# A second prefetch place of 2 MB beside an eight-slot weight ring, both places used for two rounds

## The chip, the cores and the metric

One Trainium2 chip; the kernel runs on one of its cores. The metric is the device time of one execution, in microseconds. The kernel before takes 1180.39 us (median of three runs, 1180.38 to 1183.22).

## What is computed

A decoder layer on 256 tokens of width 1024, all in float32: RMSNorm, a combined input projection, an S5 state-space mixer and an RWKV-7 time mixer side by side, an output projection, then a mixture of 32 experts (the four best per token) with clamped SwiGLU, an input embedding p that is gated by the residual, and a last RMSNorm. The part around the change, cut to its core:

```
logits = h @ router_w + router_b
top_v, top_i = top_k(logits, 4);  gates = softmax(top_v)
for every expert e, for the tokens that chose it:
    gt  = min(x @ w_gate[e] + b_gate[e], 7)
    up  = clip(x @ w_up[e] + b_up[e], -7, 7)
    act = (up + 1) * gt * sigmoid(1.702 * gt)
    out[token] += (act @ w_down[e] + b_down[e]) * gate
x = x + out
x = x + (p @ ple_w_proj) * sigmoid(rms_norm(x) @ ple_w_gate)
result = rms_norm(x) * final_g
```

Every expert's three matrices (1024 x 1024 float32, 4 MB each, 402 MB in all) are read from HBM once.

## The kernel before

**Memory.** Nearly all on-chip memory is one tensor, arena, of 47 units; a unit is 128 partitions x 1024 float32 (512 KB). un(i, n) are n units from unit i. The mixers use the units for their own data first; the expert phase takes them over as they fall free. Small tensors beside it: rec, bb, cc, lora_hidden, s5p (20 x 16 columns), power (160) and coef (256), which hold the S5 mixer's tables and are dead when the experts begin.

**Chunks and the ring.** An expert's weights come as six chunks of 2 MB (four units): two of gate, two of up, two of down, chunk c of expert e in the order in which TensorE uses them. Chunk i below counts through all experts: 0 to 191. The ring has eight slots (NSLOT) at the units of RING. Beside it there is one special place, extra, made of units 24, 25, 26 and 29, which holds chunk 8 and is used once. So nine chunks are fetched before or as the first expert begins: chunks 0 to 7 into slots 0 to 7, and chunk 8.

**Who fetches.** All these transfers are issued by SyncE, in the order written in the block for sync and then in expert_sync; its queue is in order, and a wait holds everything behind it. Ahead of the experts it issues slots 0, 4, 5 (L335), the token rows and the p projection's weights, slot 1 (L348, when the RWKV chunks are done), slots 6 and 7 (L352, on mix_rw_ready), slots 2 and 3 (L355, when the output projection is done), and three of the four units of extra (L358, when the router's logits are done). The fourth unit, 29, holds the weights of the p projection until that is done; expert_sync issues it (L1490) after chunk 12, on ple_done 4. TensorE raises the semaphore chunks_used when it has used a chunk. In expert_sync chunk i waits for chunks_used i-8 up to chunk 16 and for i-7 from then on (L1487, then the loop at L1499, then L1502), and goes to slot (i-1) mod 8. Behind the last chunk, which is fetched in two halves, come the two chunks of ple_w_gate (L1510) and the final gain (L1512).

**TensorE per expert** (expert in expert_tensor). Gate: 16 matmuls of 64 rows x 512 columns for each of two chunks, then the bias; up the same; then scatter, which adds the output y of the expert before to the four banks of outputs (4 matmuls, with the gate weights gT turned for the scatter); two transposes of the gate table pg and four of the act; gather of the next expert's tokens (4 matmuls); the down matmuls of two chunks, with the turn of the gathered rows between them. VectorE does the clamps and the product (the act stage, L1562 to L1569), ScalarE the sigmoid and the copies. Every float32 matmul runs as two passes, and the trace counts passes. For expert 0 there is more: open_outputs does the second half of the p projection for bank 1 (ple_proj(1)), waits until ScalarE has copied it (L1343), and opens the four banks with the down biases; then scatter runs on y and gT, which VectorE cleared beforehand (L1388, L1389), so that it adds zeros.

## Time and profile before

| | |
|---|---|
| median of three runs | 1180.39 us |
| the profiled execution's own time | 1182.24 us |
| its span | 1180.4 us |
| TensorE matmul busy | 1104.3 us (94%) |
| VectorE, ScalarE busy | 359.5 us (30%), 198.6 us (17%) |
| bytes moved, mean rate | 430.58 MB, 365 GB/s |
| granted clock of TensorE | 0.998 |

The span runs from the first to the last recorded instruction; the own time is the device's time for the same execution. A busy share is a mean over stages with different limits, so what a change is worth has to be read in the stage that it touches. The granted clock 0.998 is that of the full level, 2.4 GHz.

### The profile page before, as it was taken

To read this page: it belongs to the slowest core of one execution; us is meant where nothing else is said; L and a number is where in the kernel's file an instruction comes from. 1 tells how busy PE (TensorE), PEld (TensorE's weight loads), DVE (VectorE), ACT (ScalarE), POOL (GpSimd) and SP (SyncE) were. 2 spreads that over 40 slices of the span, in tenths; PEclk is the share of its full clock that TensorE was granted. 3 is DMA by queue.
4 is the path that set the end of the run, shared out by engine and by line. 5 is a ranking of instruction groups with operands and counts; after the bars stand their busy time and mean duration, and the time that the engine had idled before them with its cause. 6 is when DMAs were issued, how large, how long until landed. Compare 5 with 4: busy or idle time off the path is not lost.

```text
span 1180.4 us, 16582 instructions
## 1 busy us (share of the span) xinstructions
PE 1104.3 (94%) x7042; PEld 480.1 (41%) x7042; DVE 359.5 (30%) x745; ACT 198.6 (17%) x318; POOL 5.8 (0%) x11
## 2 busy tenths in 40 slices
PE   9999999999999999999999999999999999999987
PEld 8788974433333333333333333333333333333334
DVE  7987745312222222212111222222111111111123
ACT  6761322310110000000000000000000000000022
POOL 0100000000000000000000000000000000000000
PEclk9999999999999999999999999999999999999999
DMA  9402284899999999999999999999999999999970
GB/s 325 134 2 78 88 328 154 362 393 401 428 428 428 428 427 429 429 428 428 429 429 429 428 428 429 429 428 428 429 429 428 428 428 431 428 426 428 428 300 36
DMA packets 44844, 430.58 MB, mean 365 GB/s; under 512 B 4992, under 2 KB 15616, under 8 KB 20096
## 3 DMA queue, kind: packets, MB, share of 16 engines
q1 hardware_dynamic: 44608, 429.40, 87.2%
q8 instruction: 36, 0.59, 0.2%
q0 software_dynamic: 192, 0.52, 0.1%
q14 instruction: 8, 0.07, 0.0%
HBM read 428.86 MB, written 1.05 MB: 364 GB/s over the span
## 4 chain that ended last, share of the span: by engine, by line
PE 50%; DMA 44%; DVE 4%; ACT 1%; issue 1%; SPq 0%; DVEq 0%; ACTq 0%
PE bank L1321 34%; DMA arena<-in_exp_w_up 24%; DMA arena<-in_exp_w_gate 19%; PE bank L249 13%; PE bank L1383 1%; DVE arena L638 1%; PE bank L1632 1%; PE bank L1628 1%; DMA arena<-in_xT 0%; ACT arena L475 0%; PE bank L984 0%; DVE arena L882 0%; DVE arena L629 0%; DVE arena L632 0%; PE bank L266 0%
## 5 line engine op out<-in xcount | busy, mean ns | idle before, releaser
L1321 PE MATMUL bank<-arena 128*64 128x512 f32 (+3 forms) x3808 | 849.7, 588 | 59.1 <-DMA arena<-in_exp_w_up 52.0
L1321 PEld LDWEIGHTS bank<-arena 128*64 128x64 f32 (+3 forms) x3808 | 272.4, 140 | 591.1 <-issue 471.6
L249 PE MATMUL bank<-arena 64*64 64x64 f32 (+8 forms) x2104 | 170.7, 265 | 7.1 <-issue 3.6
L249 PEld LDWEIGHTS bank<-arena 64*64 64x64 f32 (+3 forms) x2104 | 137.0, 146 | 35.9 <-issue 18.5
L1517 ACT ACTIVATE cc<-arena 128x512 f32<-128x512 f32 x32 | 20.2, 630 | 459.7 <-DVE arena L1562 459.7
L1567 DVE TENSOR_SCALAR arena<-bank 128x512 f32<-128x512 f32 x32 | 22.1, 692 | 219.9 <-PE bank L1321 219.9
L1364 DVE TENSOR_TENSOR arena<-bank,par 128x512 f32<-128x512 f32 x32 | 22.1, 692 | 216.7 <-PE bank L1383 216.7
L1562 DVE TENSOR_SCALAR arena<-bank 128x512 f32<-128x512 f32 x32 | 22.1, 692 | 163.4 <-PE bank L1321 163.4
L1522 ACT ACTIVATE arena<-bank 128x256 f32<-128x256 f32 x32 | 12.3, 383 | 313.9 <-PE bank L1628 313.9
L1577 DVE COPY arena<-bank 128x512 f32<-128x512 f32 x32 | 22.1, 692 | 98.7 <-PE bank L1321 98.7
L1377 ACT ACTIVATE rec<-bank 128x512 f32<-128x512 f32 x32 | 34.2, 1069 | 43.0 <-PE bank L1321 43.0
L1569 DVE SCALAR_TENSOR_TENSOR arena<-arena,cc 128x512 f32<-128x512 f32 x32 | 33.8, 1056 | 1.1
L1565 DVE TENSOR_TENSOR cc<-cc,arena 128x512 f32<-128x512 f32 x32 | 22.2, 692 | 24.5 <-ACT cc L1517 24.5
L1383 PEld LDWEIGHTS bank<-con,rec 128*128 128x128 f32 x128 | 13.4, 141 | 26.2 <-issue 25.1
L1383 PE MATMUL bank<-con,rec 128*128 128x128 f32 x128 | 21.0, 286 | 0.8 <-ACT rec L1377 0.8
L1524 ACT ACTIVATE arena<-bank 128x512 f32<-128x512 f32 x32 | 19.1, 597 | 1.7
L1549 DVE TENSOR_SCALAR arena<-con,arena 128x128 f32<-128x128 f32 x64 | 19.1, 341 | 0.9 <-issue 0.8
L1632 PE MATMUL bank<-con,arena 128*128 128x128 f32 x128 | 19.2, 273 | 0.0
L1360 DVE TENSOR_SCALAR arena<-con,arena,small 128x64 f32<-128x64 f32 x64 | 17.2, 311 | 6.7 <-DVE arena L1555 6.6
L1628 PEld LDWEIGHTS bank<-con,arena 128*128 128x128 f32 x64 | 6.4, 141 | 24.3 <-issue 24.3
L1632 PEld LDWEIGHTS bank<-con,arena 128*128 128x128 f32 x128 | 15.0, 140 | 0.0
L1628 PE MATMUL bank<-con,arena 128*128 128x128 f32 x64 | 14.0, 301 | 0.0
(278 smaller groups left out, 406.8 us busy)
## 6 DMA issues: line engine op xcount, KB each, us to landing
arena<-in_exp_w_gate SPq DMA_DIRECT2D x64, 2048.0 KB, 31.9
arena<-in_exp_w_down SPq DMA_DIRECT2D x63, 2048.0 KB, 35.4
arena<-in_exp_w_up SPq DMA_DIRECT2D x63, 2048.0 KB, 34.3
arena<-in_w_in SPq DMA_DIRECT2D x8, 1024.0 KB, 12.0
arena<-in_w_out SPq DMA_DIRECT2D x4, 1024.0 KB, 6.3
arena<-in_ple_w_gate SPq DMA_DIRECT2D x2, 2048.0 KB, 33.3
arena<-in_exp_w_down SPq DMA_DIRECT2D x2, 1024.0 KB, 34.5
arena<-in_exp_w_up SPq DMA_DIRECT2D x1, 1536.0 KB, 12.8
```

Of the source, the lines that this page charges most:

```text
L249: return nc.tensor.matmul(out, lhsT, rhs, start=start, stop=stop, skip_group_check=True)
L1321: return nc.tensor.matmul(out, lhsT, rhs, start=start, stop=stop, skip_group_check=True)
L1364: nc.vector.tensor_tensor(xg[:, :, :].rearrange("p (h k) s -> p k h s", h=2), GAT[:, :].rearrange("p (k h s) -> p k h s", h=2, k=4), prm(" ...
L1377: nc.scalar.activation(by_run(xc), plain(GAT[:, :]), ACT.Copy).then_inc(s["moved"], 1)
L1383: last = nc.tensor.transpose(GAT[:, k * P:(k + 1) * P], xc[:, k * P:(k + 1) * P], ident)
L1562: ts(gt, GATE[:, :], 7.0, None, ALU.min).then_inc(s["gt_ready"], 1)
L1565: tt(sg, sg, gt, ALU.mult).then_inc(s["swish_ready"], 1)
L1567: ts(up, UP[:, :], 7.0, -7.0, ALU.min, ALU.max).then_inc(s["swish_ready"], 1)
L1569: stt(by_run(gt), plain(up), 1.0, plain(sg), ALU.add, ALU.mult).then_inc(s["act_ready"], 1)
L1577: V.tensor_copy(y, YB[:, :]).then_inc(s["y_ready"], 1)
L1628: ins = nc.tensor.transpose(YB[:, t * P:(t + 1) * P], pg[:, t, :], ident)
L1632: ins = nc.tensor.transpose(GATE[:, k * P:(k + 1) * P], gt[:, k * P:(k + 1) * P], ident)
```

## The change

- There are two special places instead of one. Place a is units 24 to 27, place b units 37, 38, 28, 29. In the first round they hold chunks 8 and 9, in the second 18 and 19. FIRST is 10, the number of places.
- Chunks 0 to 9 fill the ten places, 10 to 19 fill them again, and chunks 20 to 27 go to the eight slots. Up to chunk 27 chunk i waits for chunks_used i-9; from chunk 28 on the ring alone is used and chunk i waits for i-7, in slot (i-20) mod 8, which is (i-4) mod 8. Chunk 28 thus waits for three uses more than chunk 27.
- Units 37 and 28 of place b are fetched right behind slot 1, unit 38 behind slots 2 and 3, the whole of place a where three units of extra went, and unit 29 behind chunk 11, still on ple_done 4. Chunk 19 is fetched in two pieces of 1 MB.
- To free the units, the routing state moves: gates, ranks and counts to power, one-hot, pick and turned gates to s5p, gT to coef, pg, up and the gathered rows xc to rec, the four p projections to bb, lora_hidden and unit 40, xg and the routing scratch to unit 41, y to the place of the down bias, half of the turned rows x2T to unit 24.
- Expert 0's scatter of zeros is left out, with the clearing of gT and y; the second part of the p projection moves from open_outputs to just behind the gate bias of expert 0.
- The final gain goes to unit 43 and is fetched one use later.

The diff, cut where it only passes names on or gives tiles other columns:

```diff
-        x2T = [feat(25 + 3 * (k // 4))[:, k % 4, :] for k in range(KD)]
+        x2T = [feat(25 - k // 4)[:, k % 4, :] for k in range(KD)]
-        extra = [un(a) for a in (24, 25, 26, 29)]
+        extra = [[un(a) for a in places] for places in ((24, 25, 26, 27), (37, 38, 28, 29))]
...
-        ahead = chunk_src(NSLOT % NC, 1)
+        ple = [bb.rearrange("p m n -> p (m n)"), lora_hidden[:, :], un(40)[:, 0:512], un(40)[:, 512:1024]]
+        ahead = [chunk_src((NSLOT + i) % NC, 1) for i in range(2)]
...
                 sp.dma_start(slot(1), chunk_src(1, 0)).then_inc(chunk_in[1], 16)
+                for k, place in ((0, 37), (2, 28)):
+                    sp.dma_start(un(place), ahead[1][:, k * D:(k + 1) * D]).then_inc(extra_in[1], 16)
...
                 for c in (2, 3):
                     sp.dma_start(slot(c), chunk_src(c, 0)).then_inc(chunk_in[c], 16)
+                sp.dma_start(un(38), ahead[1][:, D:2 * D]).then_inc(extra_in[1], 16)
                 sp.wait_ge(s["logits_done"], 1)
                 sp.wait_ge(s["x2_root"], 2)
-                sp.dma_start(un(24, 3), ahead[:, 0:3 * D]).then_inc(extra_in, 16)
+                sp.dma_start(un(24, 4), ahead[0]).then_inc(extra_in[0], 16)
...
-        V.memset(gT[:, :, :], 0.0).then_inc(s["gT_ready"], 1)
-        V.memset(y, 0.0).then_inc(s["y_ready"], 1)
-        for i, name in enumerate(("actT_ready", "gT_done")):
+        for i, name in enumerate(("gT_ready", "y_ready", "actT_ready", "gT_done")):
             V.memset(st[:, 8 + i:9 + i], 0.0).then_inc(s[name], 1)
...
     def open_outputs(pe):
 
-        ple_proj(1, banks[1]).then_inc(mixer["ple_done"], 1)
         pe.wait_ge(s["ple_copied"], 4)
         for n in range(4):
-            mm(banks[n][:, :], gatesT[rows[n], :], bias_down[rows[n], :], True, False)
+            last = mm(banks[n][:, :], gatesT[rows[n], :], bias_down[rows[n], :], True, False)
+        return last
...
+    FIRST = NSLOT + len(extra)
+    def ring_slot(i):
+        return (i - 2 * FIRST) % NSLOT
...
     def expert_sync(sp):
-        for i in range(NSLOT + 1, QUAD * NC):
-            sp.wait_ge(s["chunks_used"], i - NSLOT if i <= 2 * NSLOT else i - NSLOT + 1)
-            sp.dma_start(slot((i - 1) % NSLOT), chunk_src(i % NC, i // NC)).then_inc(chunk_in[(i - 1) % NSLOT], 16)
-            if i == NSLOT + 4:
+        for i in range(FIRST, 2 * FIRST + NSLOT):
+            sp.wait_ge(s["chunks_used"], i - FIRST + 1)
+            src = chunk_src(i % NC, i // NC)
+            if i == 2 * FIRST - 1:
+                sp.dma_start(un(37, 2), src[:, 0:2 * D]).then_inc(extra_in[1], 16)
+                sp.dma_start(un(28, 2), src[:, 2 * D:4 * D]).then_inc(extra_in[1], 16)
+            elif i == 2 * FIRST - 2:
+                sp.dma_start(un(24, 4), src).then_inc(extra_in[0], 16)
+            else:
+                c = i % FIRST if i < 2 * FIRST else ring_slot(i)
+                sp.dma_start(slot(c), src).then_inc(chunk_in[c], 16)
+            if i == FIRST + 1:
                 sp.wait_ge(mixer["ple_done"], 4)
-                sp.dma_start(extra[3], ahead[:, 3 * D:4 * D]).then_inc(extra_in, 16)
+                sp.dma_start(un(29), ahead[1][:, 3 * D:4 * D]).then_inc(extra_in[1], 16)
...
+        begun = 2 * FIRST + NSLOT - QUAD * NC
         with sp.Fori(1, n_last) as q:
-            for i in range(QUAD * NC):
-                if i % NC == 0:
+            for i in range(begun, begun + QUAD * NC):
+                if i % NC == 0 or i == begun:
                     e = sp.snap((QUAD * q + i // NC) % E)
                 sp.wait_ge(s["chunks_used"], QUAD * NC * q + (i - NSLOT + 1))
-                sp.dma_start(slot((i - 1) % NSLOT), chunk_src(i % NC, e)).then_inc(chunk_in[(i - 1) % NSLOT], 16)
+                sp.dma_start(slot(ring_slot(i)), chunk_src(i % NC, e)).then_inc(chunk_in[ring_slot(i)], 16)
...
-        sp.wait_ge(s["chunks_used"], base + (2 * QUAD * NC - 5))
+        sp.wait_ge(s["chunks_used"], base + (2 * QUAD * NC - 4))
         sp.dma_start(fg[:, :], io["final_g"].to_broadcast([P, D])).then_inc(t2["fg_in"], 16)
...
                 ins.then_inc(s[done], 1)
+                if q is None and place == 0 and m == 0:
+                    ple_proj(1, banks[1]).then_inc(mixer["ple_done"], 1)
             if q is None and place == 0:
-                open_outputs(pe)
-            pe.wait_ge(s["gT_ready"], n + 1)
-            pe.wait_ge(s["y_ready"], n + 1)
-            scatter().then_inc(s["scattered"], 1)
+                open_outputs(pe).then_inc(s["scattered"], 1)
+            else:
+                pe.wait_ge(s["gT_ready"], n + 1)
+                pe.wait_ge(s["y_ready"], n + 1)
+                scatter().then_inc(s["scattered"], 1)
```

The order on SyncE from slot 1 to chunk 15, with the semaphores waited for. 128x4096 is a chunk, 128x1024 a unit. Before:

```order
L348 DMA arena<-in_exp_w_gate 128x4096 [waits state_done,y_done,u0_done]
L352 DMA arena<-in_exp_w_gate 128x4096 [waits mix_rw_ready]
L352 DMA arena<-in_exp_w_gate 128x4096
L355 DMA arena<-in_exp_w_up 128x4096 [waits out_done]
L355 DMA arena<-in_exp_w_up 128x4096
L358 DMA arena<-in_exp_w_up 128x3072 [waits x2_root,logits_done]
L1487 DMA arena<-in_exp_w_up 128x4096 [waits m_chunks_used]
L1487 DMA arena<-in_exp_w_down 128x4096 [waits m_chunks_used] x2
L1487 DMA arena<-in_exp_w_gate 128x4096 [waits m_chunks_used]
L1490 DMA arena<-in_exp_w_up 128x1024 [waits ple_done]
L1487 DMA arena<-in_exp_w_gate 128x4096 [waits m_chunks_used]
L1487 DMA arena<-in_exp_w_up 128x4096 [waits m_chunks_used] x2
```

Now:

```order
L350 DMA arena<-in_exp_w_gate 128x4096 [waits state_done,y_done,u0_done]
L352 DMA arena<-in_exp_w_up 128x1024 x2
L356 DMA arena<-in_exp_w_gate 128x4096 [waits mix_rw_ready]
L356 DMA arena<-in_exp_w_gate 128x4096
L359 DMA arena<-in_exp_w_up 128x4096 [waits out_done]
L359 DMA arena<-in_exp_w_up 128x4096
L360 DMA arena<-in_exp_w_up 128x1024
L363 DMA arena<-in_exp_w_up 128x4096 [waits x2_root,logits_done]
L1508 DMA arena<-in_exp_w_down 128x4096 [waits m_chunks_used] x2
L1511 DMA arena<-in_exp_w_up 128x1024 [waits ple_done]
L1508 DMA arena<-in_exp_w_gate 128x4096 [waits m_chunks_used] x2
L1508 DMA arena<-in_exp_w_up 128x4096 [waits m_chunks_used] x2
```

Two units move up to a place without a wait of their own, one unit to a place behind slot 3, and chunk 9 no longer waits for a use.

The order on TensorE in expert 0, from the up matmuls' first chunk (chunk_in2) to the transposes of the act. Before:

```order
L1321 MATMUL bank<-arena 64x512 [waits chunk_in2]
L1321 MATMUL bank<-arena 64x512 x7
L1321 MATMUL bank<-arena 64x512 [waits chunk_in3]
L1321 MATMUL bank<-arena 64x512 x7
L1321 MATMUL bank<-arena 64x512 [waits m_gatesT_ready,bias_split,m_picked]
L1321 MATMUL bank<-arena 64x512
L249 MATMUL bank<-arena,lora_hidden 128x512 x2
L1321 MATMUL bank<-arena 128x512 [waits m_ple_copied]
L1321 MATMUL bank<-arena 128x512 x3
L1321 MATMUL bank<-arena 128x512 [waits m_y_ready,m_gT_ready]
L1321 MATMUL bank<-arena 128x512 x3
L1628 MATMUL bank<-con,arena 128x128 [waits m_pg_ready]
```

Now:

```order
L249 MATMUL bank<-arena,lora_hidden 128x512 x2
L1327 MATMUL bank<-arena 64x512 [waits chunk_in2]
L1327 MATMUL bank<-arena 64x512 x7
L1327 MATMUL bank<-arena 64x512 [waits chunk_in3]
L1327 MATMUL bank<-arena 64x512 x7
L1327 MATMUL bank<-arena,s5p 64x512 [waits m_gatesT_ready,bias_split,m_picked]
L1327 MATMUL bank<-arena,s5p 64x512
L1327 MATMUL bank<-arena,s5p 128x512 [waits m_ple_copied]
L1327 MATMUL bank<-arena,s5p 128x512 x3
L1658 MATMUL bank<-con,rec 128x128 [waits m_pg_ready]
```

The p projection stands ahead of the up matmuls, and the four matmuls that waited for y and gT are gone.

## Rows read from the trace of the kernel before

**Rows 1.** The page, part 2: GB/s moved, in 40 equal slices of the span.
```profile
GB/s 325 134 2 78 88 328 154 362 393 401 428 428 428 428 427 429 429 428 428 429 429 429 428 428 429 429 428 428 429 429 428 428 428 431 428 426 428 428 300 36
```

**Rows 2.** The chain that ended last, in order of time: start, us, what.
```profile
471.56 35.25 DMA arena<-in_exp_w_up
...
1088.18 35.88 DMA arena<-in_exp_w_up
1124.10 5.79 PE bank L1321 x26
...
1148.73 22.36 PE bank L1321 x64
```

**Rows 3.** Windows: busy us of each engine (x count), granted clock, DMA share, GB/s.
```profile
184.00:190.00 6.00, 6.00 (x15) 2.66 (x14) 4.15 (x3) 2.94 (x4) 0.00 (x0) 1.00 0.95 344
190.00:200.00 10.00, 8.72 (x21) 3.60 (x20) 9.73 (x19) 0.00 (x0) 0.00 (x0) 1.00 0.01 3
200.00:204.00 4.00, 4.00 (x17) 2.27 (x16) 1.77 (x3) 1.88 (x5) 0.00 (x0) 1.00 1.03 336
204.00:224.00 20.00, 17.48 (x94) 10.37 (x94) 7.20 (x31) 11.40 (x29) 0.00 (x0) 1.00 1.00 427
224.00:228.00 4.00, 4.00 (x22) 1.36 (x20) 1.39 (x7) 0.00 (x0) 0.00 (x0) 1.00 0.07 28
228.00:248.00 20.00, 19.31 (x92) 6.75 (x90) 3.14 (x4) 3.27 (x5) 0.00 (x0) 1.00 1.00 410
248.00:252.00 4.00, 4.00 (x22) 1.45 (x20) 0.69 (x1) 0.00 (x0) 0.00 (x0) 1.00 0.84 258
252.00:276.00 24.00, 24.00 (x117) 8.21 (x114) 5.12 (x12) 2.68 (x4) 0.00 (x0) 1.00 0.99 414
276.00:288.00 12.00, 12.00 (x60) 4.31 (x62) 3.37 (x10) 0.02 (x1) 0.00 (x0) 1.00 0.93 356
288.00:460.00 172.00, 172.00 (x826) 60.43 (x822) 37.49 (x81) 18.73 (x28) 0.00 (x0) 1.00 1.01 428
460.00:1100.00 640.00, 588.58 (x2747) 195.68 (x2743) 128.20 (x286) 56.90 (x85) 0.00 (x0) 1.00 1.01 428
```

**Rows 4.** The timeline of SyncE's issues: start, us, engine, line, out<-in.
```profile
183.40 0.34 SPq L348 DMA_DIRECT2D arena<-in_exp_w_gate  x1
199.08 0.81 SPq L352 DMA_DIRECT2D arena<-in_exp_w_gate  x2
213.46 0.33 SPq L358 DMA_DIRECT2D arena<-in_exp_w_up  x1
227.15 0.33 SPq L1487 DMA_DIRECT2D arena<-in_exp_w_up  x1
249.64 0.33 SPq L1487 DMA_DIRECT2D arena<-in_exp_w_gate  x1
267.76 0.33 SPq L1487 DMA_DIRECT2D arena<-in_exp_w_down  x1
276.00 0.33 SPq L1487 DMA_DIRECT2D arena<-in_exp_w_gate  x1
1114.97 0.43 SPq L1512 DMA_DIRECT2D arena<-in_final_g  x1
```

**Rows 5.** The timeline of TensorE over experts 0 and 1; x counts passes.
```profile
223.45 14.39 PE L1321 MATMUL bank<-arena 128*64 128x512 f32 x68 [0.78 <-DVE arena L1364]
237.77 1.98 PE L249 MATMUL bank<-arena,lora_hidden 128*128 128x512 f32 x4
240.44 3.06 PE L1321 MATMUL bank<-arena 32*128 32x512 f32 x16 [0.69 <-ACT arena L1343]
250.12 19.74 PE L1321 MATMUL bank<-arena 128*64 128x512 f32 x92
...
276.48 19.74 PE L1321 MATMUL bank<-arena 128*64 128x512 f32 x92
```

**Rows 6.** DMA issues of the page: KB each, us to landing.
```profile
arena<-in_exp_w_up SPq DMA_DIRECT2D x63, 2048.0 KB, 34.3
```

More of the change, by code:

```diff
@@ L291, in slot @@
             return un(RING[c], RUN)
-        ahead = chunk_src(NSLOT % NC, 1)
-        clear_expert_state, rest_sync, rest_scalar, rest_vector, rest_tensor = experts(nc, io, ctx, arena, con, par, banks, ring, slot, ahead, extra, sg, xc, chunk_in, extra_in, chunk_src, p_in, ple_proj, s, logits, inv, by_run, plain, x2, bias_parts, bias_down, rbias)
+        ple = [bb.rearrange("p m n -> p (m n)"), lora_hidden[:, :], un(40)[:, 0:512], un(40)[:, 512:1024]]
+        state_tables = [a.rearrange("p m n -> p (m n)") for a in (s5p,)] + [a.rearrange("p a b n -> p (a b n)") for a in (power, coef)]
+        ahead = [chunk_src((NSLOT + i) % NC, 1) for i in range(2)]
+        clear_expert_state, rest_sync, rest_scalar, rest_vector, rest_tensor = experts(nc, io, ctx, arena, con, par, banks, ring, slot, ahead, extra, sg, rec, ple, state_tables, chunk_in, extra_in, chunk_src, p_in, ple_proj, s, logits, inv, by_run, plain, x2, bias_parts, bias_down, rbias)
         with nc.Block() as block:
@@ L1263, in _, with experts @@
                 rest_tensor(pe)
-def experts(nc, io, ctx, arena, con, par, banks, ring, slot, ahead, extra, sg, xc, chunk_in, extra_in, chunk_src, p_in, ple_proj, mixer, logits, inv, by_run, plain, x2, bias_parts, bias_down, rbias):
+def experts(nc, io, ctx, arena, con, par, banks, ring, slot, ahead, extra, sg, rec, ple, state_tables, chunk_in, extra_in, chunk_src, p_in, ple_proj, mixer, logits, inv, by_run, plain, x2, bias_parts, bias_down, rbias):
     def sb(name, shape, dt=F32):
@@ L1281, in experts @@
     HF = D // 2
-    y = un(40)[:, 0:HF]
-    xg = un(40)[:, HF:2 * HF].rearrange("p (k s) -> p k s", k=KD)
+    tables, counts, turned_gates = state_tables
+    xc, up = rec[:, 0:HF], rec[:, 0:HF]
+    pg = rec[:, HF:HF + TT * P].rearrange("p (t m) -> p t m", t=TT)
+    y = bias_down
     gt = un(41)[:, 0:HF]
-    up = un(41)[:, HF:2 * HF]
+    xg = un(41)[:, HF:2 * HF].rearrange("p (k s) -> p k s", k=KD)
     actT = un(42)[:, HF:2 * HF].rearrange("p (h k s) -> p k h s", h=2, k=4)
-    gT = un(37)[:, 0:TT * P].rearrange("p (t m) -> p t m", t=TT)
@@ L1307, in experts @@
-    nbase = un(38)[:, 425:426].bitcast(I32)
-    nlast = un(38)[:, 426:427].bitcast(I32)
+    gT = turned_gates.rearrange("p (t m) -> p t m", t=TT)
+    onehot = tables[:, 0:128].rearrange("p (t m) -> p t m", t=TT)
+    pick = tables[:, 128:160].bitcast(BF16)
+    gatesT = tables[:, 160:288]
+    st = tables[:, 288:320]
+    gates = counts[:, 0:64].rearrange("p (t e) -> p t e", t=TT)
+    rank = counts[:, 64:128].rearrange("p (t e) -> p t e", t=TT)
+    cnt, cflag = counts[:, 128:136], counts[:, 136:144]
@@ new lines, in experts @@
+    nbase = counts[:, 145:146].bitcast(I32)
+    nlast = counts[:, 146:147].bitcast(I32)
+    route = un(41)[:, 256:1024]
+    lg = route[:, 0:64].rearrange("p (t e) -> p t e", t=TT)
+    mask = route[:, 64:128].rearrange("p (t e) -> p t e", t=TT)
+    top = route[:, 128:144].rearrange("p (t e) -> p t e", t=TT)
+    topi = route[:, 144:160].bitcast(U32).rearrange("p (t e) -> p t e", t=TT)
+    topf = route[:, 160:176].rearrange("p (t e) -> p t e", t=TT)
+    ex = route[:, 176:192].rearrange("p (t e) -> p t e", t=TT)
@@ L1332, in chain @@
         return link
-    ple = [un(28 - n // 2)[:, (n % 2) * HF:(n % 2 + 1) * HF] for n in range(4)]
     PLE_ORDER = (2, 3, 0, 1)
```

65 lines of the change are left out of this document (29 added, 36 removed).

## The prediction

> **What bounds the kernel now.** I read the throughput of the transfers slice by slice first. From the eleventh slice (295 us) to the end of the expert phase every slice shows 426 to 431 GB/s [rows 1]: the transfer engines never rest, and nothing in TensorE's work changes that rate. Next the chain that ended last, in order of time: until 471 us it runs through TensorE alone, from there through transfers of expert weights with TensorE between them, as in the first piece shown and the last one, which hands over at 1124.10 us; behind it stands the tail, whose gate matmuls take 22.36 us [rows 2]. So the end is set by when the chunk that lands at 1124 lands. It is the 190th of 192 (chunk 189, the second half of the last expert's up matrix). All bytes ahead of it pass through one queue in order, so its time is the moment the stream starts, plus bytes over rate, plus every microsecond in which the stream stood still for want of a free place. The windows show where it stood still: almost nothing moves in 190 to 200, 28 GB/s in 224 to 228, 258 in 248 to 252, 414 in 252 to 276, 356 in 276 to 288, then 428 throughout [rows 3]. TensorE is busy for 172.00 us of the 172 from 288 to 460, and 588.58 of the 640 after that [rows 3]: it first lives on the buffered lead and then waits for data. One chunk of 2048 KB [rows 6] at 428.4 GB/s (between the 428 and 429 of [rows 1]) takes 4.90 us, an expert's six 29.4 us; TensorE needs 26.36 (250.12 to 276.48, [rows 5]).
>
> So one question prices this change: how much of the stream's idle time before 288 us does it fill, and does it open new idle time later. A microsecond saved on TensorE is worth something only if it releases a place that the stream waits for.
>
> **What the stream loses now.** Against 428.4 GB/s: 204 to 224: 0.07 us; 224 to 228: 3.74; 228 to 248: 0.86; 248 to 252: 1.59; 252 to 276: 0.81; 276 to 288: 2.03 [rows 3]. Together 9.1 us. The causes are in SyncE's issues [rows 4]. The special place's 1.5 MB went out at 213.46; the next chunk can only go when chunk 0 is used, at 227.15. Chunk 13 waited for the fifth use, at 249.64. Chunk 18 waited for use 11, at 276.00, a whole act stage behind use 10 at 267.76, and since chunk 17 is where the distance had fallen from nine places to eight, nothing was queued. A model with one queue, a start 1.7 us behind the issue (issue at 199.08; the 336 GB/s of 200 to 204 are 3.14 us at full rate, so data starts at 200.86, [rows 3, 4]) and 4.90 us a chunk gives a gap at each of these three places: 4.8, 1.6 and 2.0 us, 8.4 in all. The 0.8 us of 252 to 276 it doesn't explain.
>
> **The change, part by part.**
>
> 1. *Two units (1 MB) of the second special place go out right behind chunk 1, at 183.8 us.* No wait stands between (the order of SyncE). Chunk 1's data ends at 190 (344 GB/s over 184 to 190 are its 2.1 MB), and the stream then rests until 200.86 [rows 3]. 1 MB is half a chunk, 2.45 us: it fits into that rest. **Gain 2.45 us.** Nobody reads those units before the expert phase, and slots 6 and 7 still go out at 199.08.
>
> 2. *Unit 38 goes out behind slots 2 and 3, and the first special place takes 2 MB at 213.46 instead of 1.5.* The stream from 200.86 carries 6, 7, 2, 3, a quarter chunk, and a whole one: 5.25 chunks or 25.7 us, to 226.6, where before it ended at 224.1. The next data starts at 228.8 (use at 227.15 and 1.7). The gap is 2.3 us where the model had 4.8: **2.5 us saved**. The bytes are no extra ones; they come out of the work behind.
>
> 3. *Ten places until chunk 27.* Chunk i now waits for use i-9 where it waited for i-8 (from 17 on i-7). Stream from 228.8: chunks 10 to 13 and the quarter chunk of unit 29 end at 249.6. Chunk 14 now needs the fifth use, which was at 249.64 and comes at 247.5 (point 4); with 1.7 us that is 249.2, so **the 1.6 us gap is gone**, with 0.4 us to spare. Chunk 20 (use 11, at 273.9) meets a stream busy until 283.9: **the 2.0 us gap is gone**. Without point 4 the first of these would keep about 1.7 us.
>
> 4. *The first expert on TensorE.* Left out: the scatter of zeros, 8 passes of 0.214 us (92 passes in 19.74 us, [rows 5]), 1.7 us. The p projection (1.98 us) moves ahead of the up matmuls, so the 0.69 us wait for ScalarE's copy of it [rows 5] is gone too: ScalarE copies it behind the sigmoid, during the up matmuls. Uses 3 and 4 come 1.95 us later, which costs the stream nothing, as chunk 11 is queued ahead until 238.6. Uses 5 and later come 2.4 us earlier, less some 0.3, my estimate for what now shows of VectorE's act: the scatter was covering it, and the opening matmuls (3.06 less 1.7 us) and two transposes alone are short of it. I take 2.1. TensorE's own saving is worth nothing at the end, since transfers set it; it counts only through point 3.
>
> 5. *The ring falls from ten to eight at chunk 28.* This is the new wait: chunk 27 goes at use 18, chunk 28 only at use 21. Use 11 was at 276.00; use 23 is two periods of 26.36 later, 328.7; use 21 is the act stage (276.00 less 267.76, 8.24 us) and one chunk (16 passes, 3.4) before that, 317.1, and 315.0 with point 4. Chunk 27 ends at 228.8 + 18.25 x 4.90 = 318.2. Data for 28 can flow from 316.7, so it is in time by 1.5 us. Chunk 30 waits for use 23, 326.6 + 1.7 = 328.3, and 29 ends at 328.0: a gap of **0.3 us lost**. Behind it the lead of TensorE shrinks by 3 us an expert, uses come ahead of the stream's need, and no gap follows. Bounds for this step: nothing, and 2.0 us (what the same fall from nine to eight costs now).
>
> 6. *At nothing.* State in other tables: the same instructions on VectorE and ScalarE, with two memsets fewer, at about 199 us, where TensorE has its own work (8.72 us of the ten from 190, 4.00 of the four from 200, [rows 3]). up and the gathered rows share rec: the one is written after the other has been turned, as TensorE's order has it anyway. Final gain one use later (now issued at 1114.97, [rows 4]): it stands in the queue behind the last weights, of which 4.25 chunks follow the one that lands at 1124.10, so it comes by about 1145, and the tail needs it behind its gate matmuls, at 1171 [rows 2]. One more loop step on SyncE: transfers there are issued some seven chunks ahead of landing (34.3 us, [rows 6]).
>
> Row and rule differ on the small pieces. In 204 to 224 the stream crosses from one transfer to the next four times and moves 427 GB/s [rows 3], so a border costs under 0.1 us when the next one is queued. The Trainium skill (SBUF — State Buffer, The DMA setup-cost knee) says that every transfer pays a fixed 2 us or so, and to coalesce into the largest; there are three transfers more than before (eight for chunks 8, 9, 18 and 19 instead of five), which by that figure would be an estimate of 6 us of the gain. The page itself puts most of it down to completion, which a queued successor covers; the trace agrees.
>
> **The sum.** Early megabyte 2.45, first gap 2.5, second 1.6, third 2.0, less 0.3: 8.2 us; I take 8.1, since chunk 14 comes so close. The unexplained 0.8 stays. Bounds: 2.45 + 2.5 = 4.9 if the later dips stay, and 2.45 + 9.1 - 2.3 = 9.2 if all but the first gap's rest goes. The profiled execution took 1182.24 us, so the sum is 1174.1 against it; it lay 1.85 above the median of the three runs, 1180.39, and against that the forecast is **1172.3 us**, 0.7% faster. About 0.3%, 3.5 us, is what a measurement of this kernel can tell from no change.
>
> **Rivals.**
> - *The dips stay* (20%). The losses at 248 to 288 come from a queue one or two deep at each issue, not from missing places, or the fall at chunk 28 costs its 2.0 us. For it: 0.8 us that my model can't place, and margins of 0.4 and 1.5 us at chunks 14 and 28. Against: three gaps fit the issues to 0.1 us. Gain 4.9: 1175.5.
> - *The early megabyte isn't early* (3%): the change doesn't do what it says, because something holds SyncE there or the transfers run beside slots 6 and 7. Gain 8.1 - 2.45: 1174.7. Against: SyncE has nothing to wait for there.
> - *Each piece pays* (8%). Three more transfers take 2 us of the stream each. A start of 1.7 us behind an issue is in the rows, but only when the stream was empty. Gain 8.1 - 6: 1178.3, no change. This is the knee of the Trainium skill's page named above, taken literally.
> - *More* (5%): all of the dips go; 9.2 gained: 1171.2.
> - *The stream slows* (4%), the case on the other side. Chunk i now goes to slot (i-4) mod 8 instead of (i-1) mod 8, for all of the long stretch. The 186 chunks from 200.86 to the last that counts take 911 us; a rate 0.9% lower eats the 8.1 us, and from there on the kernel is slower: at 420 GB/s it loses 18 us, 1190. Against: 426 to 431 in every slice, whatever the phase between matrix and slot [rows 1].
>
> **Chances.** Forecast, a gain of 7 to 9: 60%. Faster by over 0.3% takes the forecast, the dips, the late megabyte and the larger gain: 88%; within 0.3%: 8%; slower: 4%. The range reaches from 1170.0 (the larger gain and a microsecond of scatter) to 1176.8 (the dips stay, and a microsecond), which leaves out the last two cases, 12%, and the edges.
>
> **What would show it.** In the changed profile: transfers busy at 190 to 193; 336 GB/s or so still in 200 to 204; the low window of 224 to 228 about half as deep; full rate through 248 to 288; at most a small dip at 328; chunk 14 issued at about 247.5; TensorE's first wait for weights later than 471, and the last weight transfer of the chain handing over at 1116 instead of 1124.10, with the tail behind it unchanged. Wrong would be: a dip of over 1 us at 315 to 330 (point 5), one at 247 to 252 (point 4), or a rate under 428 behind 330 us (the last rival).

## The result, and the profile after

| | before | changed |
|---|---|---|
| median of five runs each | 1183.22 us (1180.38 to 1183.46) | 1174.35 us (1172.43 to 1175.17) |
| profiled execution, own time | 1182.24 us | 1174.35 us |
| its span | 1180.4 us | 1172.6 us |

The ratio is 0.9931, with a 95% interval of 0.9917 to 0.9945: 8.1 us of the before's 1180 or so (6.5 to 9.8 by the interval), and 7.9 between the two profiled executions. The forecast was a gain of 8.1 us and a time of 1172.3. The median of before rose from 1180.39 with two more runs, both near 1183.4; its five values lie near 1180.4 and near 1183.3. The last section shows how far such differences can be followed.

The page's GB/s in 40 slices, for the changed kernel, answers to [rows 1]:

```profile
GB/s 323 138 2 43 84 369 173 395 414 428 428 425 428 426 428 427 429 429 429 428 429 429 427 428 429 429 429 429 428 429 428 428 429 429 427 427 428 428 296 36
```

The full rate begins a slice earlier; the plateau behind it is where it was, with one slice of 425. The windows answer to [rows 3] (busy us of PE, PEld, DVE, ACT, POOL, then granted clock, DMA share, GB/s):

```profile
190.00:200.00 10.00, 8.72 (x21) 3.67 (x20) 9.79 (x20) 0.00 (x0) 0.00 (x0) 1.00 0.28 111
200.00:204.00 4.00, 4.00 (x17) 2.20 (x16) 1.00 (x2) 1.95 (x5) 0.00 (x0) 1.00 0.97 340
204.00:224.00 20.00, 17.48 (x94) 10.43 (x94) 7.20 (x31) 11.36 (x29) 0.00 (x0) 1.00 1.01 426
224.00:228.00 4.00, 4.00 (x22) 1.30 (x20) 1.39 (x7) 0.00 (x0) 0.00 (x0) 1.00 0.66 283
228.00:248.00 20.00, 19.56 (x94) 6.65 (x90) 3.13 (x4) 3.28 (x5) 0.00 (x0) 1.00 1.00 410
248.00:252.00 4.00, 4.00 (x21) 1.37 (x21) 0.80 (x2) 0.00 (x0) 0.00 (x0) 1.00 0.97 369
252.00:276.00 24.00, 24.00 (x118) 8.52 (x116) 5.71 (x13) 2.69 (x4) 0.00 (x0) 1.00 1.00 422
276.00:288.00 12.00, 12.00 (x60) 4.03 (x58) 3.37 (x10) 0.63 (x1) 0.00 (x0) 1.00 1.02 431
320.00:332.00 12.00, 12.00 (x60) 4.33 (x58) 2.26 (x5) 2.06 (x3) 0.00 (x0) 1.00 1.00 422
460.00:1100.00 640.00, 592.68 (x2774) 198.51 (x2772) 127.78 (x286) 59.08 (x88) 0.00 (x0) 1.00 1.01 428
```

Read each against 428.4 GB/s, as the prediction did. 190 to 200 now moves 1.1 MB where nothing moved. 224 to 228 loses 1.36 us instead of 3.74, 228 to 248 0.86 as before, 248 to 252 0.55 instead of 1.59, 252 to 276 0.36 instead of 0.81, 276 to 288 nothing instead of 2.03, and there is a new 0.18 in 320 to 332. With 0.11 in 204 to 224 that is 3.4 us where 9.1 were lost; with the megabyte in the earlier rest (2.45) the stream stands 8.1 us ahead.

SyncE's issues answer to [rows 4]:

```profile
183.72 0.91 SPq L352 DMA_DIRECT2D arena<-in_exp_w_up  x2
199.02 0.80 SPq L356 DMA_DIRECT2D arena<-in_exp_w_gate  x2
213.40 0.33 SPq L363 DMA_DIRECT2D arena<-in_exp_w_up  x1
227.09 0.33 SPq L1508 DMA_DIRECT2D arena<-in_exp_w_down  x1
247.71 0.33 SPq L1508 DMA_DIRECT2D arena<-in_exp_w_up  x1
274.07 0.33 SPq L1508 DMA_DIRECT2D arena<-in_exp_w_up  x1
315.34 0.36 SPq L1521 DMA_DIRECT2D arena<-in_exp_w_down  x1
326.98 0.33 SPq L1521 DMA_DIRECT2D arena<-in_exp_w_gate  x1
```

These are the two early units, slots 6 and 7, place a, and chunks 10, 14, 20, 28 and 30. TensorE's timeline in expert 0 answers to [rows 5]:

```profile
230.62 1.98 PE L249 MATMUL bank<-arena,lora_hidden 128*128 128x512 f32 x4
232.54 7.09 PE L1327 MATMUL bank<-arena 128*64 128x512 f32 x32
239.46 1.46 PE L1327 MATMUL bank<-arena,s5p 128*64 128x512 bf16 x10
240.84 0.44 PE L1658 MATMUL bank<-con,rec 128*128 128x128 f32 x2
241.72 0.66 PE L1662 MATMUL bank<-con,arena 128*128 128x128 f32 x4 [0.44 <-DVE arena L1592]
```

The scatter is gone, and 0.44 us of VectorE's act shows in its place. The chain that ended last, in order of time, answers to [rows 2]:

```profile
515.62 31.33 DMA arena<-in_exp_w_gate
...
1080.79 35.40 DMA arena<-in_exp_w_up
1116.20 0.04 issue
1116.24 5.79 PE bank L1327 x26
...
1140.87 22.36 PE bank L1327 x64
```

TensorE lives on its lead 44 us longer, and the last weight transfer hands over 7.86 us earlier (1124.10 to 1116.24). Everything behind it takes what it took: 22.36 us of gate matmuls, and 24.63 us from the handover to their start, before and after.

### The profile page after: what moved, and what is told of

Read it like the earlier page. It is cut to its first block, busy times and chain, and to the rows that moved or that the text cites. A ratio compares the mean times of both kernels' runs of the same rounds, so it can differ in the third digit from the quotient of the medians.

```text
span 1172.6 us, 16567 instructions
## 1 busy us (share of the span) xinstructions
PE 1102.4 (94%) x7034; PEld 481.8 (41%) x7034; DVE 358.3 (31%) x745; ACT 199.2 (17%) x318; POOL 5.4 (0%) x11
## 4 chain that ended last, share of the span: by engine, by line
PE 52%; DMA 41%; DVE 4%; ACT 1%; issue 1%; SPq 0%; DVEq 0%; ACTq 0%
PE bank L1327 37%; DMA arena<-in_exp_w_up 21%; DMA arena<-in_exp_w_gate 20%; PE bank L249 12%; PE bank L1388 1%; DVE arena L643 1%; PE bank L1662 1%; PE bank L1658 1%; DMA arena<-in_xT 0%; PE bank L989 0%; ACT arena L480 0%; DVE arena L887 0%; DVE arena L634 0%; DVE arena L637 0%; PE bank L266 0%
## 5 line engine op out<-in xcount | busy, mean ns | idle before, releaser
L1327 PE MATMUL bank<-arena 128*64 128x512 f32 (+1 forms) x3152 | 715.2, 593 | 52.1 <-DMA arena<-in_exp_w_up 46.6
L1327 PEld LDWEIGHTS bank<-arena 128*64 128x64 f32 (+1 forms) x3152 | 227.0, 138 | 503.2 <-issue 397.9
L1327 PE MATMUL bank<-arena,s5p 128*64 128x512 f32 (+2 forms) x392 | 87.7, 532 | 1.0 <-DVE s5p L1365 1.0
L1590 DVE TENSOR_SCALAR rec<-bank 128x512 f32<-128x512 f32 x32 | 22.1, 692 | 215.6 <-PE bank L1327 215.6
L1585 DVE TENSOR_SCALAR arena<-bank 128x512 f32<-128x512 f32 x32 | 22.1, 692 | 164.3 <-PE bank L1327 164.3
L1327 PE MATMUL bank<-arena,coef 64*128 64x512 f32 x256 | 63.6, 615 | 0.8 <-DVE arena L1600 0.8
L1327 PEld LDWEIGHTS bank<-arena,s5p 128*64 128x64 f32 (+2 forms) x392 | 23.3, 128 | 43.5 <-issue 42.4
L1327 PEld LDWEIGHTS bank<-arena,coef 64*128 64x128 f32 x256 | 22.0, 186 | 36.1 <-issue 34.5
L1592 DVE SCALAR_TENSOR_TENSOR arena<-rec,cc 128x512 f32<-128x512 f32 x32 | 33.7, 1052 | 1.1
L1572 DVE TENSOR_SCALAR rec<-con,power 128x128 f32<-128x128 f32 x64 | 19.1, 342 | 0.7 <-issue 0.7
```

Source lines behind the costliest of these rows:

```text
L1327: return nc.tensor.matmul(out, lhsT, rhs, start=start, stop=stop, skip_group_check=True)
L1585: ts(gt, GATE[:, :], 7.0, None, ALU.min).then_inc(s["gt_ready"], 1)
L1590: ts(up, UP[:, :], 7.0, -7.0, ALU.min, ALU.max).then_inc(s["swish_ready"], 1)
L1592: stt(by_run(gt), plain(up), 1.0, plain(sg), ALU.add, ALU.mult).then_inc(s["act_ready"], 1)
```

## The experiments

Twelve runs follow, and their expectations speak of three theories. **Theory 1**: the time is set by the *last* moment at which the stream of weight transfers stands still, since all that comes behind flows at one rate. **Theory 2**: each rest is priced by itself, and a microsecond of a filled one counts in full, as my prediction had it. **Theory 3**: TensorE's saved work is the gain.

One measure serves for all. Executions differ by some us in when the experts begin (last section), so I take from each profile the time from the issue of slots 6 and 7 to the handover of the last weight transfer of the chain. The changed kernel has 917.22 us (199.02 to 1116.24), the kernel before 925.02 (199.08 to 1124.10). Ratios are of the runs' times to those of the kernel before, with the 95% interval.

| run | issue | handover | us between | against the changed kernel | ratio |
|---|---|---|---|---|---|
| before | 199.08 | 1124.10 | 925.02 | +7.8 | 1 |
| changed | 199.02 | 1116.24 | 917.22 | 0 | 0.9931 |
| changed, again | 197.58 | 1114.65 | 917.07 | -0.2 | 0.9935 [0.9922, 0.9948] |
| early megabyte late | 198.75 | 1116.11 | 917.36 | +0.1 | 0.9934 [0.9920, 0.9948] |
| part 4 undone | 197.66 | 1116.52 | 918.86 | +1.6 | 0.9957 [0.9943, 0.9971] |
| before with part 4 | 197.22 | 1119.70 | 922.48 | +5.3 | 0.9983 [0.9973, 0.9993] |
| fall at chunk 18 | 197.72 | 1120.62 | 922.90 | +5.7 | 0.9997 [0.9979, 1.0016] |
| nine places | 198.59 | 1120.42 | 921.83 | +4.6 | 0.9972 [0.9956, 0.9987] |
| gather twice, expert 0 | 200.76 | 1119.08 | 918.32 | +1.1 | 0.9941 [0.9917, 0.9966] |
| gather twice, experts 4 to 30 | 199.21 | 1115.85 | 916.64 | -0.6 | 0.9938 [0.9916, 0.9960] |
| three rounds | 200.40 | 1118.53 | 918.13 | +0.9 | 0.9939 [0.9926, 0.9952] |
| three rounds, halves | 206.75 | 1124.05 | 917.30 | +0.1 | 0.9936 [0.9920, 0.9952] |
| two rounds, halves | 198.57 | 1115.62 | 917.05 | -0.2 | 0.9916 [0.9892, 0.9939] |
| unintended repeat | 197.30 | 1114.29 | 916.99 | -0.2 | 0.9930 [0.9908, 0.9952] |

Three profiles of the same changed kernel lie within 0.23 us in this measure. Every other kernel has one profile, and between kernels the measure can be off by more. The handover comes when chunk 189 has landed, and how much of what is queued behind it has been moved by then differs. Windows of 45 us from the handover on, in which the queue runs empty, for the changed kernel, the gather twice in experts 4 to 30, and three rounds:

```profile
1116.24:1161.24 45.00, 42.58 (x160) 20.28 (x161) 11.34 (x18) 8.86 (x15) 0.00 (x0) 1.00 0.42 171
1115.85:1160.85 45.00, 42.58 (x160) 20.31 (x161) 11.33 (x18) 8.85 (x15) 0.00 (x0) 1.00 0.44 178
1118.53:1163.53 45.00, 42.50 (x160) 20.35 (x161) 11.27 (x18) 8.85 (x15) 0.00 (x0) 1.00 0.41 166
```

171 GB/s over 45 us are 7.7 MB still to come; 7 GB/s more are 0.3 MB, so that handover comes 0.7 us early against the stream, and the last one, with 5 less, 0.5 us late. The kernel before and the other runs have 169 to 173, except the gather twice in expert 0 (176), before with part 4 (178) and three rounds with halves (165). Why the handover shifts stays open. So for small differences I also read how far the stream itself got: its rate over the 120 us that begin 25 us behind the issue of slots 6 and 7. It is 416, 416 and 417 GB/s in the three profiles of the changed kernel; 1 GB/s there is 0.28 us. The changed kernel, the gather twice in expert 0, and in experts 4 to 30:

```profile
224.02:344.02 120.00, 119.56 (x572) 41.56 (x568) 26.06 (x61) 11.98 (x18) 0.00 (x0) 1.00 0.99 416
225.76:345.76 120.00, 119.56 (x572) 41.45 (x568) 26.07 (x61) 11.95 (x18) 0.00 (x0) 1.00 0.99 409
224.21:344.21 120.00, 119.57 (x572) 41.42 (x569) 26.07 (x61) 11.96 (x18) 0.00 (x0) 1.00 0.99 415
```

**The changed kernel again.** The first is the yardstick.

> The changed kernel again, as the measure for the other runs of this call: 1172.4 to 1175.2 us, 8 us under the kernel before; the transfers rest in 226.6 to 228.8 and for 0.3 to 0.5 us at 328, and the last weight transfer of the chain hands over at 1116.2.

917.07 us against 917.22; as expected.

**The early megabyte, late.** The two unit loads move, still ahead of the first use:

```diff
                 sp.dma_start(slot(1), chunk_src(1, 0)).then_inc(chunk_in[1], 16)
-                for k, place in ((0, 37), (2, 28)):
-                    sp.dma_start(un(place), ahead[1][:, k * D:(k + 1) * D]).then_inc(extra_in[1], 16)
...
                 sp.dma_start(un(38), ahead[1][:, D:2 * D]).then_inc(extra_in[1], 16)
+                for k, place in ((0, 37), (2, 28)):
+                    sp.dma_start(un(place), ahead[1][:, k * D:(k + 1) * D]).then_inc(extra_in[1], 16)
```

> The early megabyte (units 37 and 28) moved behind slots 2 and 3, still ahead of the first use. Theory 1 (the last gap of the stream decides, here chunk 30, which waits for use 23): the megabyte fills the rest at 226.6 to 228.8 instead of the one at 190, the gap at 328 stays, handover at 1116.2, no change against the changed kernel. Theory 2 (the sum of my prediction: the early megabyte is worth 2.45 us by itself): 2.45 us slower, handover at 1118.7. Theory 3 (TensorE's saved work is the gain): no change either.

Measured: 917.36, and a ratio of 0.9934 beside the 0.9935 of the changed kernel. Its windows show why, against those of the changed kernel above:

```profile
190.00:200.00 10.00, 8.72 (x21) 3.60 (x20) 9.79 (x19) 0.00 (x0) 0.00 (x0) 1.00 0.09 16
...
224.00:228.00 4.00, 4.00 (x22) 1.39 (x20) 1.16 (x7) 0.00 (x0) 0.00 (x0) 1.00 1.03 438
228.00:248.00 20.00, 19.57 (x96) 6.66 (x94) 3.12 (x4) 3.28 (x5) 0.00 (x0) 1.00 1.01 429
```

The megabyte that is missing at 190 fills the rest at 224 to 228. Both rests lie ahead of the first use, and all ten places are full by then either way. Theory 2 falls: the early issue by itself is worth nothing that can be seen. What falls is the price put on one rest before the run. The rests of a finished profile may well be added up, as in the section above, since the stream's end is its bytes and its rests; but filling one rest can open or fill another.

**Part 4 undone.**

```diff
     def open_outputs(pe):
+        ple_proj(1, banks[1]).then_inc(mixer["ple_done"], 1)
         pe.wait_ge(s["ple_copied"], 4)
...
-                if q is None and place == 0 and m == 0:
-                    ple_proj(1, banks[1]).then_inc(mixer["ple_done"], 1)
             if q is None and place == 0:
-                open_outputs(pe).then_inc(s["scattered"], 1)
-            else:
-                pe.wait_ge(s["gT_ready"], n + 1)
-                pe.wait_ge(s["y_ready"], n + 1)
-                scatter().then_inc(s["scattered"], 1)
+                open_outputs(pe)
+            pe.wait_ge(s["gT_ready"], n + 1)
+            pe.wait_ge(s["y_ready"], n + 1)
+            scatter().then_inc(s["scattered"], 1)
```

gT is cleared again, and unit 29 goes behind chunk 12, so that SyncE doesn't stand in front of it.

> Part 4 of the change undone alone: the scatter of zeros is back in expert 0 and the p projection stands behind the up matmuls again. Theory 1: use 5 and all later ones come 2.1 us later, so chunk 30 starts at 330.4 instead of 328.3: 2.0 us slower than the changed kernel, handover at 1118.2, and rests of 1.7 us at 250 and 0.7 us at 330. Theory 2 says the same size, by the second gap (1.6) and more of the last. Theory 3: also about 2 us slower. If only the places mattered: no change.

1.6 us slower than the changed kernel, a fifth under the expected 2.0, with the rest at 250 back (343 GB/s in 244 to 252). Over its 120 us the stream moves 409 GB/s instead of 416, which is 2.0 us. So a saving of TensorE time in expert 0 is worth nearly its full size. The times alone can't tell the two kernels apart: their intervals overlap.

**The kernel before with part 4 alone.** The same edit the other way round, on the kernel before.

> The kernel before with part 4 alone (scatter of zeros left out, p projection ahead of the up matmuls). Theory 1: chunk 18 waits for use 11, which comes 2.1 us earlier: handover at 1122.1 instead of 1124.1, 2.0 us faster than before; the gap at 249 goes and the one at 276 stays as long. Theory 2 (gaps are added up): 1.6 us. If only the places mattered: no change.

2.5 us faster than before (925.02 to 922.48; ratio 0.9983, interval 0.9973 to 0.9993). Theory 1 said 2.0, theory 2 1.6, which is too close to choose between them. 0.7 of the 2.5 are the early handover (178 against the 171 of the kernel before); over the 120 us the stream moves 404 GB/s where it moved 397, which is 2.0 us. Part 4 is thus worth about 2 us on either kernel; the places are worth the other 5 to 6.

**The fall at chunk 18.** Everything as in the changed kernel, but both places count for one round only:

```diff
-            sp.wait_ge(s["chunks_used"], i - FIRST + 1)
+            sp.wait_ge(s["chunks_used"], i - FIRST + 1 if i < FIRST + NSLOT else i - NSLOT + 1)
```

> The changed kernel, but the distance falls from ten to eight at chunk 18 instead of 28 (chunks 18 to 27 wait two uses longer), as if both places were used for one round. Theory 1: chunk 18 waits for use 11 as in the kernel before, so all of the first round's lead is lost and only part 4 is left: 6 us slower than the changed kernel (2 us faster than before), handover at 1122.2, with one rest of 6.5 us at 269 to 276. Theory 2: the first gap and the megabyte (4.9 us) and the second (1.6) are kept, the third (2.0) comes back: 2 us slower than the changed kernel. Theory 3: no change.

This is where the theories lay furthest apart: theory 1 expected +6, theory 2 +2, theory 3 nothing. Measured +5.7. Windows and issues of this run:

```profile
248.00:268.00 20.00, 20.00 (x98) 7.05 (x96) 5.12 (x12) 1.55 (x3) 0.00 (x0) 1.00 1.00 414
268.00:276.00 8.00, 8.00 (x42) 2.75 (x38) 0.69 (x1) 1.14 (x2) 0.00 (x0) 1.00 0.39 124
276.00:288.00 12.00, 12.00 (x60) 3.99 (x58) 3.37 (x10) 0.63 (x1) 0.00 (x0) 1.00 0.98 401
```

```profile
257.45 0.33 SPq L1508 DMA_DIRECT2D arena<-in_exp_w_down  x1
272.77 0.33 SPq L1505 DMA_DIRECT2D arena<-in_exp_w_gate  x1
```

Chunk 17 goes at 257.45, chunk 18 only at 272.77, on use 11, and the stream, which was ahead, rests: 268 to 276 loses 5.7 us (8 x (1 - 124/428.4)). From there on it is where the kernel before would be with part 4: 922.90 and 922.48. All that the second place had won by 227 is given back at the next fall. **Without the second round the second place is worth nothing**, and this is the plainest finding of the study.

**Nine places.** Place b's first three units are fetched only on use 1, and chunk i waits for i-8 until 25 (their three loads ahead of the experts are taken out, which is not shown):

```diff
...
+        sp.wait_ge(s["chunks_used"], 1)
+        for k, place in ((0, 37), (1, 38), (2, 28)):
+            sp.dma_start(un(place), ahead[1][:, k * D:(k + 1) * D]).then_inc(extra_in[1], 16)
         for i in range(FIRST, 2 * FIRST + NSLOT):
-            sp.wait_ge(s["chunks_used"], i - FIRST + 1)
+            sp.wait_ge(s["chunks_used"], i - FIRST + 2 if i < 2 * FIRST + NSLOT - 2 else i - NSLOT + 1)
```

> One special place instead of two in effect: place b's first three units are fetched only after use 1, chunk i waits for i-8 until chunk 25 and for i-7 from 26 on. Nine places for two rounds. Theory 1: no rest at 249 worth naming (0 to 0.9 us), none at 276, the first rest is 3.5 us: 4.1 us slower than the changed kernel, handover at 1120.3. Theory 3: no change.

4.6 us slower than the changed kernel, half a microsecond over theory 1's 4.1. A place held for two rounds is worth about what it holds when the first use comes: one chunk, which takes 4.90 us.

**The gather twice in expert 0, and in experts 4 to 30.** The same added work (8 passes, same result) at two places of the program:

```diff
-                gather()
+                gather(2 if q is None and place == 0 else 1)
```

```diff
-                gather()
+                gather(1 if q is None else 2)
```

> The changed kernel with the gather of the next expert's tokens done twice in expert 0 (same result, 8 passes more, 1.7 us of TensorE). Theory 1: all uses from the fifth on 1.7 us later, chunk 30 starts 1.7 us later: 1.7 us slower, handover at 1117.9. Theory 3 (TensorE's work counts as work): 1.7 us too; it is told apart by the next run.

> The gather done twice in experts 4 to 30 instead (27 x 1.7 = 46 us of TensorE's work added), none in the first four. Theory 1: chunk 30 waits for a use of expert 3, everything later has slack: no change, handover at 1116.2, TensorE's waits for data shorter by 46 us. Theory 3: 46 us slower, or at least the part that fell into TensorE's own stretch until 515 us, some 15 us.

In expert 0 it costs 1.1 us by the handover (expected 1.7). Chunk 30 goes 1.72 us later after slots 6 and 7 (330.44 - 200.76 against 326.98 - 199.02), and the stream is behind by 7 GB/s over its 120 us, or 2.0 us; the handover then comes 0.5 us early against the stream (176 against 171). So the stream did move as theory 1 said, and a little over half a microsecond is lost in the measure. In 27 later experts, 46 us of added work in all, it costs nothing: 916.64, 0.6 less, which is the 0.7 of its early handover. Two more windows of that run:

```profile
288.00:460.00 172.00, 172.00 (x825) 60.37 (x822) 36.69 (x80) 16.20 (x25) 0.00 (x0) 1.00 1.01 426
460.00:1100.00 640.00, 627.52 (x2983) 217.55 (x2981) 127.92 (x286) 60.97 (x91) 0.00 (x0) 1.00 1.01 428
```

TensorE is busy 627.52 us of 640 where it was 592.68, and the stream moves its 428 GB/s as before. Theory 3 falls. Work on TensorE counts in expert 0, ahead of the use that the last held-up chunk waits for, and not at all in experts 4 to 30, behind it. It is free there because TensorE stays the faster side: its 26.36 us an expert with 1.7 more are still under the stream's 29.4. Where between expert 0 and expert 4 the border lies isn't shown; the run meant for it (the last one) didn't do what it should.

**Three rounds.**

```diff
     def ring_slot(i):
-        return (i - 2 * FIRST) % NSLOT
+        return (i - ROUNDS * FIRST) % NSLOT
...
-        for i in range(FIRST, 2 * FIRST + NSLOT):
+        for i in range(FIRST, ROUNDS * FIRST + NSLOT):
...
-        for place in range(QUAD):
+        for place in range(PEELED * QUAD):
             expert(None, place, NC * place)
```

with ROUNDS 3, PEELED 2, TensorE's loop from 2, and the final gain in unit 20.

> Both places used for three rounds; the distance falls at chunk 38; eight experts instead of four are written out ahead of TensorE's loop. Theory 1: the gap of 0.3 to 0.5 us at 328 goes and none comes at 365: handover at 1115.8, 0.4 us faster than the changed kernel, hardly to be told from it by the times.

A miss: 0.9 us slower than the changed kernel in the profile, where 0.4 less was expected; the times (0.9939) can't tell. 0.5 of it is the late handover (166 against 171). The page counts 0.66 MB of instructions fetched instead of 0.59, which at the stream's rate would be 0.2 us. The stream itself is where it was, 416 GB/s over its 120 us, so neither a loss nor the expected 0.4 shows in it.

**Halves.** Chunks 10 and 14 are fetched in two pieces, the first as soon as half of chunk 0 or of chunk 4 has been used:

```diff
         for i in range(FIRST, ROUNDS * FIRST + NSLOT):
+            if i in HALVED:
+                sp.wait_ge(half_used, 2 + HALVED.index(i) + 1)
+                sp.dma_start(slot(i % FIRST)[:, 0:2 * D], chunk_src(i % NC, i // NC)[:, 0:2 * D]).then_inc(half_in, 16)
...
+                    if q is None and place == 0 and m == 0 and k == RUN // 2 - 1:
+                        ins.then_inc(half_used, 1)
```

> As the one before, and chunks 10 and 14 are fetched in halves, the first as soon as TensorE has used half of chunk 0 and of chunk 4, so that the stream restarts 1.7 us earlier after the first fill. Theory 1: the rest at 226.6 shrinks from 2.3 to 0.6 us, small ones of 0.2 to 0.5 us at 232 and 253: handover at 1114.7, 1.5 us faster than the changed kernel (about 9.5 us under the kernel before). If pieces of 1 MB cost the stream something of their own: no gain.

> The changed kernel (two rounds) with chunks 10 and 14 in halves. From the issue of slots 6 and 7 to the handover of the last weight transfer the changed kernel takes 917.2 us. Theory 1 (the last rest of the stream decides; it is chunk 30's, bound to use 23): the rest at 227 shrinks by 1.7 us and the one at 328 grows by as much: 917.2, no change. Theory 2 (rests are added up): 915.5.

With three rounds it was to be 1.5 us faster than the changed kernel, and by the handover it is level with it: a miss. It is 0.8 us faster than three rounds without halves, where 1.1 was expected, and its stream moves 420 GB/s over the 120 us instead of 416, so it is 1.1 us ahead; the handover doesn't show that, coming late against the stream (165 against 171).

With two rounds: 917.05, no change. Windows of this run first, then those of the changed kernel; 223.57 and 224.02 are both 25 us behind the issue of slots 6 and 7:

```profile
223.57:231.57 8.00, 8.00 (x37) 2.66 (x32) 2.08 (x8) 0.56 (x1) 0.00 (x0) 1.00 0.91 311
248.00:252.00 4.00, 4.00 (x20) 1.29 (x18) 1.10 (x2) 0.00 (x0) 0.00 (x0) 1.00 0.95 403
320.00:340.00 20.00, 20.00 (x100) 7.18 (x100) 4.21 (x12) 2.68 (x4) 0.00 (x0) 1.00 1.00 413
```

```profile
224.02:232.02 8.00, 8.00 (x38) 2.65 (x32) 2.09 (x8) 0.56 (x1) 0.00 (x0) 1.00 0.82 311
320.00:340.00 20.00, 20.00 (x100) 7.05 (x98) 4.45 (x12) 2.69 (x4) 0.00 (x0) 1.00 1.00 420
```

The first rest did not shrink: 311 GB/s over these 8 us in either kernel, where 1.7 us less of rest was expected. The first half goes out 1.72 us before the second, but while the two halves pass, the stream is below its rate (295 GB/s in 228 to 232, against 336 in the changed kernel). What did change is small: 248 to 252 loses 0.24 us instead of 0.55, and 320 to 340 loses 0.72 instead of 0.39, so what is won ahead of chunk 30 is waited away at it. That agrees with theory 1, but since the first rest stayed as long, the run is no test of theory 2's 915.5. In the run with three rounds the same 8 us move 355 GB/s against 315 without halves, 0.7 us won of the expected 1.7. Why the halves run slowly there stays open.

No kernel of the study is clear of the changed one. The ratio 0.9916 of the run with two rounds is the lowest, but its interval holds the changed kernel's, and the measure within the profile is level.

**An edit that did nothing.** The last run was to add the same gather in expert 3:

```diff
-                gather()
+                gather(2 if q is None and place == QUAD - 1 else 1)
```

> The changed kernel with the gather done twice in expert 3, ahead of its down matmuls and so ahead of use 23. Theory 1: chunk 30 goes out 1.7 us later: 918.6 to 918.9 from the issue of slots 6 and 7 to the handover, against 917.2, though the same work in the 27 experts behind cost nothing. If the first gap alone decided: 917.2.

In expert, place counts chunks (0, 6, 12, 18), not experts, so the condition is never true and the kernel is the changed one. Chunk 30 goes out 127.96 us after slots 6 and 7 in both. The expectation is unanswered; the run counts as a third profile of the changed kernel, 916.99.

## Why the prediction was right, point by point

- **Total.** Forecast 8.1 us; 7.9 between the profiled executions, 8.1 by the ratio. The time itself came out at 1174.35 where 1172.3 was forecast: the gain was taken off 1180.39, a median of three runs, and five runs have theirs at 1183.22. Taken off the profiled execution it would have been 1174.1.
- **What bounds the kernel.** Right: no experiment moved the time clear of its scatter except by moving the stream, and 46 us of TensorE work were free.
- **Points 1 and 2, the early megabyte (2.45) and the first gap (2.5).** Their sum, one chunk, is right; taken apart they are wrong. Late, the megabyte fills the first gap instead, and nothing is lost. So the rival "the early megabyte isn't early" was mispriced: it would have given the same time as the forecast, not 1174.7. The step that failed is the one that priced a rest by itself.
- **The lower bound, too.** "The dips stay" was given a gain of 4.9 us, as if what is won at the first rest could be kept while a later one stays. With the fall at chunk 18, where the rest at 276 stays in just that way, the gain is 2.1 us (925.02 to 922.90), nearly all of it part 4's. The sum came out right because hardly any rest is left behind those that were filled, and point 5 had worked that out, with its gap of 0.3 and its margin of 1.5 us.
- **Point 3, ten places until chunk 27.** Use 5 was expected at 247.5 and chunk 14 went at 247.71; chunk 20 was expected at 273.9 and went at 274.07. 0.55 us remained at 248 to 252, where 0.4 to spare were forecast. It cost nothing in the end, because a later rest took its place.
- **Point 4, expert 0.** I took 2.1 us for use 5; it came 1.9 earlier (249.64 to 247.71), with 0.44 us of VectorE's act showing where I had 0.3. Its worth by experiment is 1.6 to 2.5 us by the handover, and 2.0 by the stream on either kernel: about a quarter of the whole gain, though I wrote only that the second gap "would keep about 1.7".
- **Point 5, the fall from ten to eight.** Chunk 28 was expected at 315.0 and went at 315.34, chunk 30 at 326.6 and 326.98; 0.18 us are lost in 320 to 332 and 0.39 in 320 to 340, where 0.3 was forecast. What I did not see is its rank. This is the rest that everything ahead is measured against: the gain is the distance by which the last rest moved. Chunk 18's data began at 277.7 in the kernel before, and twelve chunks later, at 336.5, would have been chunk 30's turn; it now begins at about 328.7 (326.98 and the same 1.7). The difference is 7.8 us, without any sum over gaps.
- **The 0.8 us that I couldn't place** in 252 to 276 halved to 0.36 by itself. Its cause stays open.
- **The start of 1.7 us.** It is a sum, not a pause: the rows of the kernel before, where chunk 9 is issued at 227.15, show no bytes until 228.00 and the first right after it, and then a rate that climbs; together that counts as 1.7 us. "Data starts at 200.86" is to be read in the same way.

```profile
227.50:228.00 0.50, 0.50 (x6) 0.15 (x4) 0.00 (x0) 0.00 (x0) 0.00 (x0) 1.00 0.00 0
228.00:228.25 0.25, 0.25 (x4) 0.03 (x2) 0.00 (x0) 0.00 (x0) 0.00 (x0) 1.00 3.12 524
```

- **Row against rule.** The three more transfers cost the stream nothing that shows: 204 to 224, where unit 38 passes, moves 426 GB/s against 427. The two early units pass where the stream would have rested, so a cost of theirs couldn't show. The Trainium skill (SBUF — State Buffer, The DMA setup-cost knee) has a fixed 2 us or so for every transfer, most of it completion latency; this trace shows no such cost where the next transfer is queued. The halves of chunk 10 are the exception. Issued into a queue that had nearly run empty, they gave back there all or more than half of what their early issue should have won.

## What to carry to other kernels

When a stream of transfers bounds the end, look for the last moment at which it stands still and for the event that it waits for there; earlier rests count only as far as they would move that moment. A prefetch place pays about one chunk if it is kept until the uses come early enough for the shorter distance as well, and its gain is given back if the distance falls before that. Saving work on the consumer pays ahead of that event, and nothing behind it as long as the consumer stays faster than the stream.
